# The recurrent block's order of products, scans and outputs in a two-model forward pass

## What is computed

```
gate, xr = split(x @ w_in)                     # 1024 + 1024 columns
xr = causal_depthwise_conv(xr, 4 taps) + b
r = sigmoid(xr @ gate_a + b)   i = sigmoid(xr @ gate_x + b)   # block diagonal, 8 blocks of 128
a = exp(-8 r softplus(-a_param))
h[t] = a[t] h[t-1] + sqrt(1 - a[t]^2) * (i xr)[t]
out = (h * gelu(gate)) @ w_out
```

## Time and profile before

| what | value |
|---|---|
| median of 3 runs | 2808.48 us |
| the profiled execution | 2808.25 us |
| its span | 2806.5 us |
| TensorE busy | 2781.8 us (99%) |
| VectorE, ScalarE, GpSimd busy | 1248.7, 1237.1, 1232.8 us (44% each) |
| recurrent stage on TensorE | about 666 to 818 us of the span |

### The profile page before, as it was taken

The page is one execution under the profiler, slowest core; times in us unless marked ns, Lnnn a source line. Parts: engine busy times, 40 slices in busy tenths (PEclk is TensorE's granted clock), DMA queues, the critical chain, the costliest instruction groups (busy, mean ns, idle before and its releaser), DMA issues.

```text
span 2806.5 us, 32448 instructions
## 1 busy us (share of the span) xinstructions
PE 2781.8 (99%) x12950; PEld 2263.8 (81%) x12950; DVE 1248.7 (44%) x2089; ACT 1237.1 (44%) x1805; POOL 1232.8 (44%) x549
## 2 busy tenths in 40 slices
PE   9999999999999999999999999999999999999998
PEld 8876888888778888887777888888877778888887
DVE  5666551534765525327666432021266674420112
ACT  4665442444754334334674443143345744442331
POOL 4222444444554444443455444444434564444443
PEclk9999999999999999999999999999999999999999
DMA  4211332333223322332222323323322223333332
GB/s 152 91 68 61 98 99 91 104 98 98 90 76 105 98 97 92 104 98 83 76 68 90 98 93 97 96 98 98 105 91 74 63 90 90 98 98 98 98 98 75
DMA packets 74726, 259.25 MB, mean 92 GB/s; under 512 B 9856, under 2 KB 9856, under 8 KB 74576
## 3 DMA queue, kind: packets, MB, share of 16 engines
q1 hardware_dynamic: 73280, 255.08, 28.6%
q10 hardware_dynamic: 1296, 2.10, 0.2%
HBM read 254.95 MB, written 2.13 MB: 92 GB/s over the span
## 4 chain that ended last, share of the span: by engine, by line
PE 94%; DVE 2%; ACT 2%; POOL 1%; issue 1%; DMA 0%; SPq 0%; DVEq 0%; POOLq 0%; ACTq 0%
PE ps L442 27%; PE ps L444 27%; PE ps L443 27%; PE ps L508 2%; PE ps L538 2%; PE ps L564 1%; PE ps L521 1%; PE ps L566 1%; PE ps L565 1%; PE ps L490 1%; PE ps L492 1%; PE ps L491 1%; PE ps L453 1%; POOL w_lo L2007 1%; ACT w_hi L924 0%
## 5 line engine op out<-in xcount | busy, mean ns | idle before, releaser
L2007 POOL TENSOR_TENSOR w_lo<-raw,w_hi 128x1024 fp32r<-128x1024 f32 x469 | 1133.4, 2419 | 1470.9 <-ACT w_hi L924 1470.9
L442 PE MATMUL ps<-xs,w_hi 128*128 128x512 f32 x2176 | 862.0, 396 | 1.6 <-DVE xs L1408 1.6
L444 PE MATMUL ps<-xs,w_lo 128*128 128x512 f32 x2176 | 847.2, 389 | 0.0
L443 PE MATMUL ps<-xs,w_hi 128*128 128x512 f32 x2176 | 847.1, 389 | 0.0
L924 ACT ACTIVATE w_hi<-raw 128x1024 fp32r<-128x1024 f32 x470 | 494.6, 1054 | 651.4 <-PE ps L444 612.8
L442 PE MATMUL ps<-hid,w_hi 128*128 128x512 f32 x1316 | 515.6, 392 | 7.2 <-POOL w_lo L2007 2.9
L444 PE MATMUL ps<-hid,w_lo 128*128 128x512 f32 x1316 | 513.0, 390 | 0.0
L443 PE MATMUL ps<-hid,w_hi 128*128 128x512 f32 x1316 | 512.7, 390 | 0.0
L442 PEld LDWEIGHTS ps<-xs,w_hi 128*128 128x128 f32 x2176 | 408.5, 188 | 96.6 <-issue 8.1
L443 PEld LDWEIGHTS ps<-xs,w_hi 128*128 128x128 f32 x2176 | 408.7, 188 | 88.7 <-issue 5.3
L444 PEld LDWEIGHTS ps<-xs,w_lo 128*128 128x128 f32 x2176 | 408.5, 188 | 85.7
(11 more groups left out here) (232 smaller groups left out, 2578.5 us busy)
## 6 DMA issues: line engine op xcount, KB each, us to landing
raw<-in_weights SPq DMA_DIRECT2D x470, 512.0 KB, 3.5
btab<-in_rel SPq DMA_DIRECT2D x8, 256.0 KB, 3.6
out<-tmp ACTq DMA_DIRECT2D x8, 256.0 KB, 2.0
hT<-in_x SPq DMA_DIRECT2D x3, 512.0 KB, 7.0
btab<-in_heads SPq DMA_DIRECT2D x6, 256.0 KB, 3.9
tmp<-in_heads SPq DMA_DIRECT2D x6, 256.0 KB, 3.9
common<-in_fixed SPq DMA_DIRECT2D x1, 642.0 KB, 10.4
hT<-in_x SPq DMA_DIRECT2D x2, 256.0 KB, 3.8
```

The lines of the kernel that those rows point to most:

```text
L442: pe.matmul(banks[bank][:], wh, rh, start=(k == 0), stop=False)
L443: pe.matmul(banks[bank][:], wh, rl, start=False, stop=False)
L444: last = pe.matmul(banks[bank][:], wl, rh, start=False, stop=(k == len(specs) - 1))
L2007: gp.tensor_tensor(w_lo[:, n % NPAIR, :], raw[:, n % NRAW, :], w_hi[:, n % NPAIR, :].bitcast(F32), ALU.subtract).then_inc(*w_low.tick(n))
```

## The change

1. TensorE runs the input product of a tile ahead of its Gelu product: `rec_x(c)`, then `rec_1(c - 1)`, then `rec_g(c)`. ScalarE and GpSimd make the weight slabs in that order; ScalarE makes the slab of `rec_g(c)` behind the high part of tile c.
2. The scans come three tiles back (they came four back). VectorE runs that of tile c - 3 behind the low part of tile c where c is odd, and ahead of tile c's input scaling where c is 4 or 6. The factor from Sqrt is multiplied up in its bank for all tiles, and the scan of tiles 6 and 7 is written into the bank too.
3. Outputs of tiles 6 and 7 are multiplied and split by VectorE (`rec_y`, `rec_y_low`), with ScalarE's high part between; GpSimd does tiles 0 to 5.
4. The output product starts with k = 0 to 3, in the order of outputs 0, 1, 3, 4, 5, 2; `rec_1(7)` stands behind output 0. The Gelu of tile 7 is made late on ScalarE, between outputs 4 and 5.

```diff
             for c in range(8):
-                rec_0(c)
-                if c:
+                rec_x(c)
+                if c == 0:
+                    root(2)
+                else:
                     rec_1(c - 1)
+                rec_g(c)
...
+            for o in rec_order:
+                rec_out(o, 0, 4)
+                if o == 0:
+                    rec_1(7)
+            for k in (4, 5):
+                for o in rec_order:
                     rec_out(o, k, k + 1)
```

ScalarE after:

```diff
+            for c in range(8):
+                batch = (c - 3, c - 2) if c in (3, 5, 7) else ()
+                if c == 7 or c in (2, 4, 6):
+                    rec_gate(c - 1)
+                for b in batch:
+                    rec_exp(b)
+                weights(("rec_x", c))
                 if c == 0:
                     root(2)
+                for b in batch:
+                    rec_root(b)
+                if c in (1, 3, 5):
+                    rec_gate(c - 1)
+                if c in (4, 6):
+                    rec_4(c - 4)
                 if c:
                     weights(("rec_a", c - 1))
                     weights(("rec_i", c - 1))
                 rec_in(c)
                 if c:
                     rec_1(c - 1)
                     rec_t(c - 1)
                 rec_high(c)
+                weights(("rec_g", c))
+                if c in (4, 6):
+                    rec_4(c - 3)
+            rec_exp(6)
+            weights(("rec_out", 0))
             weights(("rec_a", 7))
             weights(("rec_i", 7))
             rec_1(7)
+            weights(("rec_out", 1))
             rec_t(7)
+            rec_exp(7)
+            weights(("rec_out", 3))
+            rec_4(4)
+            rec_root(6)
+            rec_root(7)
             rec_decay(6)
+            rec_decay(7)
+            weights(("rec_out", 4))
+            rec_gate(7)
+            weights(("rec_out", 5))
             rec_4(5)
+            weights(("rec_out", 2))
             rec_4(6)
```

VectorE after (`rec_2` is the first multiplication on the decay, `rec_3` the rest up to the scan; the tensor_scalar on `t` is the "decay" operation for tiles 0 to 5):

```diff
+            def rec_2(c):
                 e, t, gi = ring(c)
                 V.wait_ge(act, ("rec_u", c))
+                ve.scalar_tensor_tensor(out=t, in0=e, scalar=1.0, in1=t, op0=ALU.add, op1=ALU.mult).then_inc(
+                    *vec.tick(("rec_1e", c)))
...
                 ve.tensor_tensor(u, gi, u, ALU.mult).then_inc(*vec.tick(("rec_v", c)))
+                if c < 6:
+                    V.wait_ge(vec, ("rec_1e", c))
+                    ve.tensor_scalar(t, t, -1.0, 1.0, ALU.mult, ALU.add).then_inc(*vec.tick(("rec_decay", c)))
                 V.wait_ge(vec, ("rec_v", c))
                 ve.scalar_tensor_tensor(out=u, in0=e, scalar=1.0, in1=u, op0=ALU.add, op1=ALU.mult).then_inc(
...
+                ve.tensor_tensor_scan(att[:, 8 + c, :] if c < 6 else u, t, u, 0.0, ALU.mult, ALU.add).then_inc(
+                    *vec.tick(("rec_scan", c)))
...
             for c in range(8):
+                if c in (4, 6):
+                    rec_2(c - 3)
+                    rec_3(c - 3)
+                scale(2 * (c % 2) + 1, ("rec_x", c), 2, ("rec_x", c))
+                if c in (3, 5, 7):
+                    rec_2(c - 3)
+                rec_taps(c)
+                if c:
+                    rec_1(c - 1)
+                rec_low(c)
+                if c in (3, 5, 7):
+                    rec_3(c - 3)
                 scale(2 * (c % 2), ("rec_g", c), 2, ("rec_g", c))
+            rec_2(5)
             rec_1(7)
+            rec_3(5)
+            rec_2(6)
+            rec_2(7)
+            rec_3(6)
+            rec_y(6)
+            rec_3(7)
+            rec_y(7)
+            rec_y_low(6)
+            rec_y_low(7)
```

GpSimd after:

```diff
             for c in range(8):
+                if c in (4, 6):
                     rec_3(c - 4)
                 weights(("rec_x", c))
+                if c in (4, 6):
+                    rec_4(c - 4)
                 if c:
                     weights(("rec_a", c - 1))
                     weights(("rec_i", c - 1))
+                if c in (4, 6):
+                    rec_3(c - 3)
+                weights(("rec_g", c))
+                if c in (4, 6):
+                    rec_4(c - 3)
+            weights(("rec_out", 0))
             weights(("rec_a", 7))
             weights(("rec_i", 7))
+            rec_3(4)
+            weights(("rec_out", 1))
+            weights(("rec_out", 3))
+            rec_4(4)
+            weights(("rec_out", 4))
+            rec_3(5)
```

More of the change, by code:

```diff
@@ L690, in tensor, with rec_x, rec_g @@
             network(0, 1)
[L693 to L700, removed]
+            def rec_x(c):
+                bank = 2 * (c % 2) + 1
+                linear(bank, ("rec_x", c), mat("rec_w_in", 0, 1024 + P * c), xr, x_chunk(2))
+                free[bank] = (taps, ("rec", c))
+            def rec_g(c):
+                bank = 2 * (c % 2)
+                linear(bank, ("rec_g", c), mat("rec_w_in", 0, P * c), xr, x_chunk(2))
+                free[bank] = (act, ("rec_g", c))
             def rec_1(c):
@@ L1169, in rec_t, with rec_exp, rec_root @@
                 ac.activation(t, e, ACT.Tanh, bias=sp8[:, c:c + 1], scale=sp8[:, c:c + 1]).then_inc(*act.tick(("rec_t", c)))
[L1171 to L1180, removed]
-            def rec_4(c):
-                A.wait_ge(pool, ("rec_h", c))
-                take_high(hid[:, c, :], tmp[:, 4 + c % 4, :], ("rec_y", c))
-            roots_of = {3: (0, 1), 5: (2, 3), 7: (4, 5)}
+            def rec_exp(c):
+                e = ring(c)[0]
+                A.wait_ge(act, ("rec_t", c))
+                ac.activation(e, e, ACT.Exp, bias=s1[:, c:c + 1], scale=s1[:, c:c + 1]).then_inc(*act.tick(("rec_e", c)))
+            def rec_root(c):
+                if c >= 2:
+                    A.wait_ge(vec, ("rec_scan", c - 2))
+                ac.activation(banks[6 + c % 2][:], ring(c)[1], ACT.Sqrt, scale=0.25).then_inc(*act.tick(("rec_u", c)))
+            def rec_4(c):
+                if c < 6:
+                    A.wait_ge(pool, ("rec_h", c))
+                    take_high(hid[:, c, :], tmp[:, 4 + c % 4, :], ("rec_y", c))
+                else:
+                    A.wait_ge(vec, ("rec_h", c))
+                    take_high(hid[:, c, :], banks[c][:], ("rec_y", c))
             def rec_decay(c):
@@ L1711, in vector, with rec_taps @@
             network(0, 1)
[L1714 to L1717, removed]
+            def rec_taps(c):
+                xc, ps = att[:, 8 + c, :], banks[2 * (c % 2) + 1]
                 V.wait_ge(act, ("rec_x", c))
@@ L1738, in rec_1, with rec_3 @@
                                         op1=ALU.mult).then_inc(*vec.tick(("rec_g", c)))
-            def rec_3(c):
+            def rec_2(c):
                 e, t, gi = ring(c)
                 V.wait_ge(act, ("rec_u", c))
[L1745 to L1757, removed]
+                ve.scalar_tensor_tensor(out=t, in0=e, scalar=1.0, in1=t, op0=ALU.add, op1=ALU.mult).then_inc(
+                    *vec.tick(("rec_1e", c)))
+            def rec_3(c):
                 e, t, gi = ring(c)
@@ L1768, in rec_last @@
                     *vec.tick(("rec_w", c)))
-                if c == 5:
-                    V.wait_ge(vec, ("rec_1e", c))
-                    ve.tensor_scalar(t, t, -1.0, 1.0, ALU.mult, ALU.add).then_inc(*vec.tick(("rec_decay", c)))
+                if c < 6:
                     V.wait_ge(vec, ("rec_decay", c))
@@ L2036, in gpsimd @@
             low_done["n"] += 1
-            through(("rec_g", 0))
+            through(("rec_x", 0))
             for c in range(8):
[L2039 to L2042, removed]
+                if c in (4, 6):
                     rec_3(c - 4)
                 weights(("rec_x", c))
+                if c in (4, 6):
+                    rec_4(c - 4)
                 if c:
```

90 lines of the change are left out of this document (25 added, 65 removed).

## The result

| | before | after |
|---|---|---|
| median, us | 2808.7 (2808.1 to 2809.99, 10 runs) | 2817.07 (2814.88 to 2818.19, 10 runs) |
| the profiled execution, us | 2808.25 | 2817.51 |
| its span, us | 2806.5 | 2815.7 |
| stage on TensorE (root product to next block), us | 671.51 to 818.45 = 146.9 | 672.37 to 826.87 = 154.5 |

The kernel after takes 1.0029 times as long (1.0019 to 1.0039): slower by 0.3%, against a forecast of 2815.0. Of the 9.2 us between the spans 7.6 lie in the stage that the change touches.

A forecast was written before the change was run, and what follows sets the result against it. TensorE, busy 99%, bounds the kernel, so only its waits or slow running count. New waits move the next block from 818.45 to 824.3: 2808.25 + 5.9 = 2814.1, plus 0.9 for low clock gives 2815.0 us; range 2803 to 2819.

The forecast's parts named there:

- A: TensorE's wait for the slab of `rec_g(0)`, made only behind tile 0's high part; loss 1.35 us, 1.5 with restart.
- h3: Start of ScalarE's high part of tile 3 (the number is the tile's), predicted at 715.2 us.
- B: TensorE's wait for slab 12 (`rec_a(4)`), made behind tile 4's high part; loss 2.6 us with the restart.
- C: TensorE's wait at `rec_a(6)` for the low part of tile 6; loss 4.2 us.
- D: TensorE's wait at `rec_a(7)` for the low part of tile 7; loss 3.3 us.
- E: TensorE's wait at output 2 for the late Gelu of tile 7; loss 4.2 us.
- The exclusion: GpSimd's `w_lo` and VectorE's all-SBUF operations exclude each other, first wins; the odd turns' decay ends 2.1 us late.
- Exp to tanh: Three changes between tanh and Exp on ScalarE before the Gelu of tile 7: priced at nothing, otherwise 1 to 2 us.
- the low clock: TensorE's granted clock falling to the 1.2 GHz level behind a wait; half a fall taken, +0.9 us.
- Rival 1: The decays go first in the even turns, each winning 2.1 us: 2810 us; chance 0.22.
- rival 2: The change works: no decay is held and TensorE sets the pace, 2801.4 us; chance 0.15.
- Rival 3: Low clock behind each of B to E delays slabs and gates ScalarE waits for: 2818 us; chance 0.13.

The follow-up runs named there:

- e1_swap: The changed kernel with VectorE's decay (tensor_scalar) ahead of the bank multiplication instead of behind it; 2806.58 us, 0.9997 of before.
- e5_actdecay: The changed kernel with the decays of tiles 0 to 5 made by ScalarE instead of VectorE; 2806.34 us, 0.9993 of before.
- e7_turn7: The changed kernel with decay first, `rec_g(0)` slab and tile 7's Gelu early, plus tile 7's high part ahead of Sqrt 4 and 5; 2804.59 us.
- e3_gate7: The changed kernel with ScalarE making the Gelu of tile 7 right behind its third tanh, both Exp behind it; 2814.24 us, 1.0020 of before.
- e2_slab: The changed kernel with ScalarE making the slab of `rec_g(0)` ahead of the first tile's tap; 2814.89 us, 1.0022 of before.
- e4_poolout: The changed kernel with outputs of tiles 6 and 7 back on GpSimd and their scans written to SBUF; 2818.06 us, 1.0034 of before.

## Why the prediction was right

2817.07 us lies 2.1 above the forecast, in its range, and on the side given the largest chance. All five waits came at their places and for their reasons; only the clock was mis-sized.

| step | predicted, us | measured, us |
|---|---|---|
| A, TensorE idle | 1.35 | 1.27 |
| h3 from the stage's start | 43.7 | 43.84 |
| h4 | 60.7 | 60.75 |
| B, idle | 2.5 | 2.33 |
| h5 | 75.1 | 74.98 |
| h6 | 92.1 | 91.89 |
| C, loss | 4.2 | 2.12, behind a low stretch |
| h7 | 104.9 | 104.58 |
| D, loss | 3.3 | 2.79 |
| E, the Gelu's end | 122.8 | 122.8 |
| E, loss | 4.2 | 2.68, behind a low stretch |
| next block starts | 152.8 | 154.5 |

**The exclusion.** B and C hung on who is first by 0.2 us. The decay came 0.21 us behind the `w_lo` in the odd turn, as predicted, and 0.19 in the even one (0.20), and lost in five of six cases in full (2.45 to 2.49 us; the last, which began at 786.44, 0.85 behind its `w_lo`, took 1.85). e1_swap and e5_actdecay take the collisions away in two ways, and B and C go in both. The turns, from the start of one high part to the next, show where the time was:

| turn | predicted, us | after | e1_swap | e5_actdecay |
|---|---|---|---|---|
| h3 to h4 | 17.0 | 16.91 | 13.04 | 12.38 |
| h4 to h5 | 14.35 | 14.23 | 14.24 | 14.23 |
| h5 to h6 | 17.0 | 16.91 | 13.04 | 12.39 |
| h6 to h7 | 12.8 | 12.69 | 12.69 | 12.70 |

So the collisions cost 3.9 us in each of two turns, and the last one 1.4 us between h7 and the end of E (18.3 us after, 16.9 in e1_swap). D isn't theirs: it is the last turn, 12.7 us long in all three against 9.5 us of TensorE's work, as the prediction had it. It is shorter in e1_swap and e5_actdecay because TensorE no longer waits at `rec_a(6)` and so comes to `rec_a(7)` later after h6, and it goes when e7_turn7 takes the roots and a table load out of that turn.

**The chain.** Its six points (h3 to h7 and the Gelu's end) are right to 0.3 us over 123, since the engines' orders are fixed and each row repeats. TensorE's own state between waits didn't matter: C and E came out smaller than forecast by 2.1 and 1.5 us, because a low stretch behind B and D had already taken 1.9 us each, and the ends of the waits stayed where the chain put them. Two slips of arithmetic in it are small: A's own terms give 684.70 - 683.41 = 1.29 us, not 1.35 (measured 1.27), and the terms of turn 5 add up to 14.26, not 14.35.

**Outputs 6 and 7** didn't bind, as said. The free edits (the scan into a bank, the added table load ahead of the next root) cost nothing: behind E no wait follows.

**Exp to tanh.** The tanh at 780.07 follows the Exp at 778.42 with no ACT_TABLE_LOAD between them, nor ahead of the two changes from tanh to Exp beside it (776.25 to 778.42, 781.52 to 782.36; the next load is at 786.05, for Sqrt). The price of nothing taken for the three changes of function was right. The Trainium skill (ScalarE: Activation LUTs, Table sets) puts tanh into Exp's set; by that rule the trace agrees.

**What failed.** One term of the sum, the low clock: it was put at half a fall behind E, 0.9 us. The trace shows three falls, and that behind E cost its full price: from the end of E it is 31.66 us to the next block where 44 units need 29.9. So the term is 0.8 us short. The other 1.7 of the 2.5 us between 2815.0 and the profiled 2817.5 lie outside the stage (0.86 before it, 0.8 behind it) and aren't put down to the change. The forecast's 2815.0 also lies 2.1 us below the median.

**The rivals.** Rival 1 (the decays of the even turns win) and rival 2 (none is held) didn't come true. e1_swap makes rival 2's condition nearly true (five of six decays take 0.42 to 0.43 us, the last 0.92), and its 2806.6 us lie 5.2 above rival 2's 2801.4: E, which rival 2 took as small, stayed whole (2.92 us) and had a fall behind it, and A and D stayed too. Rival 3's number, 2818, is nearer to 2817.07 than the forecast's, and the time alone can't tell the two apart; the trace can. Rival 3 wanted falls that delay ScalarE's slabs and gates, but those behind B and D were taken up by C and E and delayed nothing (h5 and h7 are on time). The prediction's count of seven collisions, in rival 2, is one more than the six decays of the program.

## What to carry to other kernels

When two engines exclude each other on SBUF, lay out the start of each instruction of the pair to 0.1 us before moving anything: the one that starts second waits for the whole of the first, and exchanging it with a neighbour that reads a bank can be worth more than a whole reordering (9 us here, for two lines). With programs written out by hand, follow the chain between engines, not the busy shares: engines that are busy 44% set the pace here. A wait removed may be gone for good (B and C in e1_swap, nearly all of E in e3_gate7) or come back as another one further on (e2_slab, e7_turn7); which of the two follows from what is next on the chain. Where a turn is set by another engine, as turns 5 and 7 by ScalarE, a shorter VectorE gives nothing in it. Put what TensorE needs next ahead of what it needs later on every engine that makes both.

## What was not expected of the hardware

The exclusion reaches further than the decays. GpSimd's product (722.56, 1.29 us) held `rec_2` (722.98) to 724.40, 0.55 us behind its end; in e1_swap, too, `rec_2` took 1416 ns in the mean, against 0.68 undisturbed, and no edit was tried that frees it.

What makes the granted clock fall behind a wait stays open. After, it fell behind waits of 2.33, 2.68 and 2.79 us and not behind 1.27 and 2.12; before, behind one of 2.54 and not behind one of 2.90. The length of the wait doesn't decide it: B is 2.33 us long in e2_slab too and there the clock stayed at 1.00, C is 2.08 us long in e4_poolout and there it fell (0.50 in 766.1 to 768), and it stayed at 1.00 behind 2.74 us in e5_actdecay and behind 3.19 us in e7_turn7. The price of a fall, when nothing behind it waits anyway, can be read from the end of E to the end of the stage, 44 units or 29.9 us of work: with a fall it is 31.66 us (after and e1_swap), 32.34 (e4_poolout) and 32.83 (e2_slab), without one 30.05 (e5_actdecay). So a fall cost 1.6 to 2.8 us. Stage times of single executions that differ by less than this don't order two kernels. Whether such falls are why executions of one kernel differ by up to 6 us here isn't shown.
